# Attention blocks of a fused transformer pair: where a pair's scores, VectorE's maxima and the bias rows stand in their queues

## The chip, the cores and the metric

The kernel runs on one core of one Trainium2 chip. The metric is device time in microseconds (us) of one execution, the median of several. The core has TensorE (PE; its weight loads are listed as PEld), VectorE (DVE), ScalarE (ACT), GpSimd (POOL) and the SyncE queue (SP). Each takes its own queue of instructions in order, and they release each other by semaphores.

## The reference, cut to what matters

Two transformer blocks run one after the other on a sequence of S = 1024 rows of width D = 1024. The second block has a mixer of two halves: a dilated attention (8 heads of width 64) and a diagonal state-space mixer (32 groups of 16 channels, 64 complex states each). The change lies in this mixer alone:

```
for window, dilation in ((128, 1), (512, 4), (2048, 16)):        # dilated_attention
    s = einsum(q, k) * 64 ** -0.5 + bias                         # bias = -slope[h] * distance, masked
    m = max(s); p = exp(s - m); denom = sum(p)
    o = einsum(p, v) / denom;  lse = m + log(denom)
out = sum over branches of softmax(lse) * o

bu = einsum(u, b_bar)                                            # s5_mixer
x_t = a_bar * x_(t-1) + bu_t
y = real(einsum(x, c)) + d_skip * u;  y = gelu(y) * sigmoid(gelu(y) @ w_glu + b_glu)
```

The kernel computes the mixture of the three branches as one softmax: a key that lies in one, two or three of the branches gets a bias of 0, log 2 or log 3 more. So one score matrix, one row maximum and one sum per head are enough.

## The kernel before, in words

The sequence has NT = 8 tiles of 128 rows. A block `n` of the attention is one head and one tile `i` of 128 queries against the `i+1` key tiles up to it, so it is 128 to 1024 wide. There are NA = 64 blocks. `block_of` orders them: heads in pairs, so blocks 2m and 2m+1 are the same tile of two heads, and the tiles of a pair of heads in the order 0, 1, 4, 5, 2, 3, 6, 7. Eight blocks are called a batch here. A batch with tiles 0, 1, 4, 5 is a short batch (blocks of 128, 256, 640 and 768 columns, two of each), one with tiles 2, 3, 6, 7 a long one (384, 512, 896 and 1024). They take turns: short, long, short, and so on, four of each; I call them A0, B0, A1, B1 to A3, B3. Blocks are numbered 0 to 7 within a batch. Four blocks that share an output bank form a group; a batch has two.

One block passes through these steps:
- `scores_pair` (TensorE, L1745) writes the scores of two blocks into banks 0 to 3. It waits for `at_m`, the maxima of the pair before, since these read the same banks.
- `maximum` (VectorE, L1759) adds the head's bias row, writes the negated scores `sco` and their row minimum `stats`, and signals `at_m`. It waits for its scores (`at_s`) and for the turns of the block three before (`at_tr`), which read the same slot of `sco`.
- the exponential (ScalarE, L1843), then `transposes` (TensorE, L1777), the turns of the 128x128 pieces, and `rest` (ScalarE, L1834), which copies them out as `probT` (`at_pt`).
- `values` (TensorE, L1804) multiplies a finished group's `probT` by V into bank 6. The work on a group is cut into four parts, one in each of the next four blocks; the last signals `at_pv`.
- `inverses` (VectorE, L1864 and L1865) takes 1/sum of a group's four blocks and spreads it over 64 columns as `rdw` (`at_r`). `factors` (TensorE, L1787) turns `rdw` into bank 6. `finish` (VectorE, L1872 and L1874) copies that out as `rdb` and multiplies the group's output by it into `att_o` (`at_o`). `factors` of a group waits for its own `inverses` and for `finish` of the group before, whose bank it overwrites.
- `head_bias` (VectorE, L1731) writes one 1024-wide bias row for a head of the next pair.

Between them stand the steps of the state-space mixer: `ssm_step_pe` (TensorE) in block 0 and 1 of a batch turns inputs (L1452), in 2 and 3 multiplies (L1419), in 5 and 6 prepares the next batch (L1460, L1452), and in block 7 multiplies twelve times (L1432 to L1434). VectorE has products in blocks 2 and 3 (L1377, L1379), an add and four scans in block 4 (L1383, L1386), and two products in block 5 (L1394, L1396). ScalarE copies the turns out (L1495) and, behind block 7, the result (L1487).

No scheduler is involved: the order in each queue is the order in which the three loops over `n` in `att_pe`, `att_act` and `att_dve` are written. Up to now TensorE's loop issues the scores of the next pair at the start of each even block, and VectorE's loop issues, at the start of a group, `finish`, then `inverses`, then the maximum, and a bias row behind the maxima of both blocks of tile 5.

Of the kernel before, what the change touches and what calls it, by code (L numbers as in the profile page):

```python
# [8 lines left out]
NT = S // P  # L9
# [9 lines left out]
N_HEADS = 8  # L19
# [25 lines left out]
def program(nc, x, p, stream, cols, rows, gate_mats, pool_mats, inv_count, ssm_g, ssm_bc, x_mid, ssm_mid, att_mid, out):  # L45
# [7 lines left out]
    with ctx:  # L53
# [1626 lines left out]
        ot_hi, ot_lo = sem("ot_hi"), sem("ot_lo")  # L1680
        NA = N_HEADS * NT
        NQ = NA // 4
        BIAS_AT = 5
        TILE_ORDER = (0, 1, 4, 5, 2, 3, 6, 7)
        TURNED_AT = {6: 0, 4: 0, 2: 4 * S, 0: 4 * S}

        def block_of(n):

            pair, r = divmod(n, 2 * NT)
            return 2 * pair + r % 2, TILE_ORDER[r // 2]  # L1690
# [36 lines left out]
        def head_bias(dve, h):  # L1727
            both = dl0 if h < 2 else dl
            if h == 2:
                dve.wait_ge(dl_in, 16)  # L1730
            nc.vector.scalar_tensor_tensor(out=bias_of(h), in0=both[:, 0:S], scalar=-2.0 ** (-(h + 1.0)),  # L1731
                                           in1=both[:, S:2 * S], op0=ALU.mult, op1=ALU.add).then_inc(dve_chain, 1)
            chained["dve"] += 1
            return chained["dve"]
# [15 lines left out]
        def maximum(dve, n, made):  # L1750
            h, i = block_of(n)
            w = (i + 1) * P
            if i == 0:
                dve.wait_ge(dve_chain, made)
            dve.wait_ge(at_s, n + 1)
            if n >= 3:
                dve.wait_ge(at_tr, n - 2)
            b = 2 * (n % 2)
            nc.vector.tensor_tensor_reduce(out=scored(n)[:, 0:w],  # L1759
                                           in0=ps[:, b:b + 2, :].rearrange("p a b -> p (a b)")[:, 0:w],  # L1760
                                           in1=bias_of(h)[:, S - w:S], scale=-1.0, scalar=3e38, op0=ALU.add,
                                           op1=ALU.min, accum_out=nm_[:, n:n + 1]).then_inc(at_m, 1)
# [5 lines left out]
        def att_pe(pe):  # L1768
            def transposes(n):
                i = block_of(n)[1]  # L1770
                pe.wait_ge(at_e, n + 1)
                if n:
                    alone = turn_bank(n) and turn_bank(n - 1)
                    if n > 1 or not alone:
                        pe.wait_ge(at_pt, n - 1 if alone else n)
                for k in range(i + 1):
                    last = nc.tensor.transpose(ps[:, (turn_bank(n) or 4) + k // 4, (k % 4) * P:(k % 4 + 1) * P],  # L1777
                                               scored(n)[:, k * P:(k + 1) * P], ident[:, :])
                last.then_inc(at_tr, 1)

            def factors(q):

                pe.wait_ge(at_r, q + 1)
                if q:
                    pe.wait_ge(at_o, q)
                for a in range(2):
                    nc.tensor.transpose(ps[:, 6, (2 + a) * P:(3 + a) * P],  # L1787
                                        rdw[:, q % 2, 2 * a:2 * a + 2, :].rearrange("p a b -> p (a b)"), ident[:, :])

            def values(q, part):  # L1790

                h, t0 = block_of(4 * q)
                if t0 == 0:
                    steps = [(0, 0, 1, True, True), (0, 1, 2, True, False), (1, 1, 2, False, True)]
                else:
                    steps = [(0, 0, 2, True, False), (t0 + 1, 1, 2, False, False)]
                    steps += [(k, 0, 2, False, k == t0) for k in range(1, t0 + 1)]
                n = len(steps)
                for i in range(part * n // 4, (part + 1) * n // 4):
                    k, a, b, first, last = steps[i]  # L1800
                    if i == 0:
                        pe.wait_ge(at_pt, 4 * q + 4)
                    for r in range(2):
                        ins = nc.tensor.matmul(ps[64 * r:64 * r + 64, 6, a * P:b * P],  # L1804
                                               V[:, k, (h + r) * HEAD_DIM:(h + r + 1) * HEAD_DIM],
                                               turned(q, r)[:, a:b, k, :], start=first, stop=last)
                    if i == n - 1:
                        ins.then_inc(at_pv, 1)

            for n in range(NA):  # L1810
                if n % 2 == 0 and n + 2 < NA:
                    scores_pair(pe, n // 2 + 1)
                if n == 0:
                    pe.wait_ge(u_out, GT)
                transposes(n)
                if n % 4 == 0 and n:
                    factors(n // 4 - 1)
                if n == 0:
                    ssm_turn_pe(pe, 0, 0)
                ssm_step_pe(pe, n)  # L1820
                if n >= 4:
                    values(n // 4 - 1, n % 4)
            factors(NQ - 1)
            for part in range(4):
                values(NQ - 1, part)
# [32 lines left out]
        def att_dve(dve):  # L1858
            link = lambda ins: link_dve(dve, ins)

            def inverses(q):

                dve.wait_ge(at_e, 4 * q + 4)
                link(nc.vector.reciprocal(rd_[:, 4 * q:4 * q + 4], den_[:, 4 * q:4 * q + 4]))  # L1864
                nc.vector.tensor_copy(rdw[:, q % 2, :, :], rd_[:, 4 * q:4 * q + 4].unsqueeze(2).to_broadcast(  # L1865
                    [P, 4, HEAD_DIM])).then_inc(at_r, 1)

            def finish(q):

                h, t0 = block_of(4 * q)  # L1870
                dve.wait_ge(at_pv, q + 1)
                nc.vector.tensor_copy(rdb[:, :], ps[:, 6, 2 * P:4 * P]).then_inc(at_d, 1)  # L1872
                dve.wait_ge(at_d, q + 1)
                nc.vector.tensor_tensor(OT[:, h // 2, t0 * P:(t0 + 2) * P], ps[:, 6, 0:2 * P], rdb[:, :],  # L1874
                                        ALU.mult).then_inc(at_o, 1)

            made = {}
            for n in range(NA):
                if n % 4 == 0 and n >= 8:
                    finish(n // 4 - 2)  # L1880
                if n % 4 == 0 and n:
                    inverses(n // 4 - 1)
                if n + 2 < NA:
                    maximum(dve, n + 2, made.get(block_of(n + 2)[0], 0))
                h, i = block_of(n + 2)
                if i == BIAS_AT and h + 2 < N_HEADS:
                    dve.wait_ge(at_m, n + 3)
                    made[h + 2] = head_bias(dve, h + 2)
                ssm_step_dve(dve, n)
                ssm_rest_dve(dve, n)  # L1890
            finish(NQ - 2)
            inverses(NQ - 1)
            lo_of(dve, glu_unit(0))
            finish(NQ - 1)
            lo_of(dve, glu_unit(1))
# [462 lines left out]
```

## Time and profile before

| | |
|---|---|
| Time, median of 3 runs | 3159.32 us (3157.42 to 3162.17) |
| The profiled execution | 3157.16 us, span 3155.3 us |
| Busy in the span | PE 3036.2 us (96%), PEld 2470.5 (78%), DVE 1376.3 (44%), ACT 869.7 (28%), POOL 411.8 (13%) |
| Granted TensorE clock, mean | 0.989 of full speed |
| The attention loop | about us 2088 to 2286 of the span |

A row of a timeline is a stretch of like instructions of one engine: its start in us from the start of the span, its length, the engine, the line, out<-in, shapes and count; in brackets how long the engine was idle before it and which instruction ended that. Matmuls are pipelined, so a row's length runs a little past the start of the next row.

### The profile page before, as it was taken

What the parts mean: (1) busy time and instruction counts of PE and PEld (TensorE: products, weight loads), DVE (VectorE), ACT (ScalarE), POOL (GpSimd) and SP (SyncE); (2) the same over time, 40 slices, a digit from 0 to 9 for tenths busy, and PEclk for the clock granted to TensorE, in tenths of its full rate; (3) what the DMA queues carried; (4) which work ended last, traced back from release to release, by engine and by line L of the source; (5) the groups of instructions that cost most, each with busy time, mean ns of one, the idle gap of its engine ahead of it and who ended that gap; (6) DMA issues with size and microseconds to landing.
All of it is one profiled execution on the core that took longest, in us unless ns stands there. A gap on an engine that the chain in (4) does not pass through costs nothing. (4 is left out here: it accounts for less than half of the span.)

```text
span 3155.3 us, 36156 instructions
## 1 busy us (share of the span) xinstructions
PE 3036.2 (96%) x13904; PEld 2470.5 (78%) x13904; DVE 1376.3 (44%) x1715; ACT 869.7 (28%) x1313; POOL 411.8 (13%) x1004
## 2 busy tenths in 40 slices
PE   7999999999998989999999999999998999999998
PEld 5767888888886768888888877876677888888886
DVE  5653444444446353433343354335546333333336
ACT  6523211222113252111211133135644211121112
POOL 0001000000000000788870010011100000000000
PEclk9999999999999999999999999999999999999999
DMA  3112111111112022122221132212122111111113
GB/s 125 40 61 80 61 43 44 53 53 53 40 41 67 27 74 67 65 80 87 94 97 40 47 114 87 82 60 71 56 91 105 65 41 47 47 60 47 40 47 127
DMA packets 54405, 206.93 MB, mean 66 GB/s; under 512 B 7216, under 2 KB 7984, under 8 KB 52000
## 3 DMA queue, kind: packets, MB, share of 16 engines
q1 hardware_dynamic: 38592, 140.53, 13.3%
q0 software_dynamic: 15712, 65.02, 5.6%
q8 instruction: 68, 1.11, 0.1%
q14 instruction: 33, 0.27, 0.0%
HBM read 173.15 MB, written 31.20 MB: 65 GB/s over the span
## 5 line engine op out<-in xcount | busy, mean ns | idle before, releaser
L126 PE MATMUL ps<-region_a,region_b 128*128 128x512 f32 x1664 | 658.0, 395 | 18.1 <-DVE region_a L221 9.8
L128 PE MATMUL ps<-region_a,region_b 128*128 128x512 f32 x1664 | 649.9, 391 | 0.0
L127 PE MATMUL ps<-region_a,region_b 128*128 128x512 f32 x1664 | 649.8, 391 | 0.0
L815 DVE TENSOR_TENSOR acc<-acc,ps 128x1024 f32<-128x1024 f32 x288 | 350.9, 1219 | 332.2 <-PE ps L128 332.2
L126 PE MATMUL ps<-region_b,region_a 128*128 128x512 f32 x1088 | 432.6, 398 | 17.3 <-DVE region_b L121 10.0
L127 PE MATMUL ps<-region_b,region_a 128*128 128x512 f32 x1088 | 428.8, 394 | 0.0
L128 PE MATMUL ps<-region_b,region_a 128*128 128x512 f32 x1088 | 428.6, 394 | 0.0
L121 DVE TENSOR_TENSOR region_b<-raw,region_b 128x1024 fp32r<-128x1024 f32 x176 | 218.0, 1254 | 395.3 <-ACT region_b L117 395.1
L126 PEld LDWEIGHTS ps<-region_a,region_b 128*128 128x128 f32 x1664 | 314.2, 189 | 86.3 <-DVE region_b L121 7.3
L128 PEld LDWEIGHTS ps<-region_a,region_b 128*128 128x128 f32 x1664 | 313.7, 189 | 65.8
L127 PEld LDWEIGHTS ps<-region_a,region_b 128*128 128x128 f32 x1664 | 314.2, 189 | 64.8 <-issue 1.7
L126 PE MATMUL ps<-region_b 128*128 128x512 f32 x896 | 351.8, 393 | 3.8 <-DVE acc L815 2.4
L128 PE MATMUL ps<-region_b 128*128 128x512 f32 x896 | 349.4, 390 | 0.0
L127 PE MATMUL ps<-region_b 128*128 128x512 f32 x896 | 349.4, 390 | 0.0
L126 PEld LDWEIGHTS ps<-region_b,region_a 128*128 128x128 f32 x1088 | 215.7, 198 | 61.6 <-issue 10.3
L128 PEld LDWEIGHTS ps<-region_b,region_a 128*128 128x128 f32 x1088 | 215.6, 198 | 41.2
L127 PEld LDWEIGHTS ps<-region_b,region_a 128*128 128x128 f32 x1088 | 215.6, 198 | 39.5
L117 ACT ACTIVATE region_b<-raw 128x1024 fp32r<-128x1024 f32 x176 | 181.4, 1050 | 162.1 <-DMA raw<-stream 130.9
L726 ACT ACTIVATE rtmp<-ps 128x512 f32<-128x512 f32 x88 | 52.7, 599 | 628.2 <-PE ps L128 628.1
L121 DVE TENSOR_TENSOR region_a<-raw,region_a 128x1024 fp32r<-128x1024 f32 x74 | 89.5, 1224 | 256.1 <-ACT region_a L117 256.1
L126 PEld LDWEIGHTS ps<-region_b 128*128 128x128 f32 x896 | 168.8, 188 | 40.6 <-DVE acc L815 3.7
L128 PEld LDWEIGHTS ps<-region_b 128*128 128x128 f32 x896 | 168.6, 188 | 35.3
(290 smaller groups left out, 3204.5 us busy)
## 6 DMA issues: line engine op xcount, KB each, us to landing
raw<-stream SPq DMA_DIRECT2D x252, 512.0 KB, 3.3
ssm_row<-ssm_mid POOLq DMA_DIRECT2D x8, 1632.0 KB, 7.7
x_mid<-acc POOLq DMA_DIRECT2D x24, 512.0 KB, 3.0
ssm_mid<-made_osc POOLq DMA_DIRECT2D x8, 1024.0 KB, 4.3
ssm_mid<-made_out POOLq DMA_DIRECT2D x8, 608.0 KB, 3.3
acc<-x SPq DMA_DIRECT2D x8, 512.0 KB, 8.2
rold<-x POOLq DMA_DIRECT2D x16, 256.0 KB, 3.4
old_a<-x_mid POOLq DMA_DIRECT2D x8, 512.0 KB, 7.2
```

Of the source, the lines that this page charges most:

```text
L117: nc.scalar.activation(slot[:, 0, :], raw[:, odd, :], ACT.Copy).then_inc(hi_done, 1)
L121: nc.vector.tensor_tensor(slot[:, 1, :], raw[:, odd, :], slot[:, 0, :].bitcast(f32), ALU.subtract).then_inc(unit_ready, 1)
L126: nc.tensor.matmul(psum, lhs(0), rhs(0), start=first, stop=False)
L127: nc.tensor.matmul(psum, lhs(0), rhs(1), start=False, stop=False)
L128: return nc.tensor.matmul(psum, lhs(1), rhs(0), start=False, stop=last)
L726: nc.scalar.activation(rtmp[:, half, :], ps[:, up_bank(c, j, half), :], ACT.Silu).then_inc(F.sem["ge"], 1)
L815: nc.vector.tensor_tensor(acc[:, t, :], acc[:, t, :], src, ALU.add).then_inc(F.sem["de"], 1)
```

## The change

Three edits in the two loops:
- TensorE: the scores that used to stand at the start of blocks 0 and 2 of a batch now stand one block earlier, behind the turns of block 7 and of block 1 (`EARLY`), and so in front of that block's state-space step. Those at the start of blocks 4 and 6 stay. `factors` moves behind the state-space step.
- VectorE: at the start of a group the maximum of block n+2 comes first, then `inverses`, then `finish`.
- VectorE: the two bias rows for the next pair of heads leave the middle of the short batch. One now stands in block 7 of the short batch, the other in block 0 of the long one.

```diff
@@ -1680,7 +1680,8 @@
         ot_hi, ot_lo = sem("ot_hi"), sem("ot_lo")
         NA = N_HEADS * NT
         NQ = NA // 4
-        BIAS_AT = 5
+        BIAS_AT = (7, 8)
+        EARLY = (1, 7)
         TILE_ORDER = (0, 1, 4, 5, 2, 3, 6, 7)
         TURNED_AT = {6: 0, 4: 0, 2: 4 * S, 0: 4 * S}
 
@@ -1808,16 +1809,18 @@
                         ins.then_inc(at_pv, 1)
 
             for n in range(NA):
-                if n % 2 == 0 and n + 2 < NA:
+                if n % 2 == 0 and n + 2 < NA and (n == 0 or (n - 1) % NT not in EARLY):
                     scores_pair(pe, n // 2 + 1)
                 if n == 0:
                     pe.wait_ge(u_out, GT)
                 transposes(n)
-                if n % 4 == 0 and n:
-                    factors(n // 4 - 1)
+                if n % 2 and n + 3 < NA and n % NT in EARLY:
+                    scores_pair(pe, (n + 3) // 2)
                 if n == 0:
                     ssm_turn_pe(pe, 0, 0)
                 ssm_step_pe(pe, n)
+                if n % 4 == 0 and n:
+                    factors(n // 4 - 1)
                 if n >= 4:
                     values(n // 4 - 1, n % 4)
             factors(NQ - 1)
@@ -1876,16 +1879,18 @@
 
             made = {}
             for n in range(NA):
+                if n + 2 < NA:
+                    maximum(dve, n + 2, made.get(block_of(n + 2)[0], 0))
+                if n % 4 == 0 and n:
+                    inverses(n // 4 - 1)
                 if n % 4 == 0 and n >= 8:
                     finish(n // 4 - 2)
-                if n % 4 == 0 and n:
-                    inverses(n // 4 - 1)
-                if n + 2 < NA:
-                    maximum(dve, n + 2, made.get(block_of(n + 2)[0], 0))
-                h, i = block_of(n + 2)
-                if i == BIAS_AT and h + 2 < N_HEADS:
-                    dve.wait_ge(at_m, n + 3)
-                    made[h + 2] = head_bias(dve, h + 2)
+                pair, r = divmod(n, 2 * NT)
+                if r in BIAS_AT and 2 * pair + 2 < N_HEADS:
+                    if pair:
+                        dve.wait_ge(at_m, 2 * NT * pair)
+                    h = 2 * pair + 2 + BIAS_AT.index(r)
+                    made[h] = head_bias(dve, h)
                 ssm_step_dve(dve, n)
                 ssm_rest_dve(dve, n)
             finish(NQ - 2)
```

The order of VectorE's queue in the middle (block 4) of a long batch, before. `rdb` and `att_o` are `finish`, `stats<-stats` and `rdw` are `inverses`, `sco` is the maximum of block 6, `m1b` and `yb` the state-space step:

```order
L1872 COPY rdb<-ps 128x256 [waits at_pv]
L1874 TENSOR_TENSOR att_o<-ps,rdb 128x256 [waits at_d]
L1864 RECIPROCAL stats<-stats 128x4 [waits at_e]
L1865 COPY rdw<-stats 128x256 [waits dve_chain]
L1759 ISA sco,stats<-ps,bias_g 128x1024 [waits at_tr,at_s]
L1759 ISA stats 128x1
L1383 TENSOR_TENSOR m1b<-m1b,m2b 128x512 [waits s5_m]
L1386 SCALAR_TENSOR_TENSOR yb<-rho,m1b 128x128 [waits dve_chain]
L1386 SCALAR_TENSOR_TENSOR yb<-rho,m1b 128x128 x3
```

and now:

```order
L1760 ISA sco,stats<-ps,bias_g 128x1024 [waits at_tr,at_s]
L1760 ISA stats 128x1
L1867 RECIPROCAL stats<-stats 128x4 [waits at_e]
L1868 COPY rdw<-stats 128x256 [waits dve_chain]
L1875 COPY rdb<-ps 128x256 [waits at_pv]
L1877 TENSOR_TENSOR att_o<-ps,rdb 128x256 [waits at_d]
L1383 TENSOR_TENSOR m1b<-m1b,m2b 128x512 [waits s5_m]
L1386 SCALAR_TENSOR_TENSOR yb<-rho,m1b 128x128 [waits dve_chain]
L1386 SCALAR_TENSOR_TENSOR yb<-rho,m1b 128x128 x3
```

The maximum is in front of the four instructions of the group, and `inverses` in front of `finish`.

VectorE's queue at the start (block 7 of the short batch, then 0 and 1) of a long batch, before:

```order
L1759 ISA sco,stats<-ps,bias_g 128x384 [waits at_tr,at_s]
L1759 ISA stats 128x1
L1872 COPY rdb<-ps 128x256 [waits at_pv]
L1874 TENSOR_TENSOR att_o<-ps,rdb 128x256 [waits at_d]
L1864 RECIPROCAL stats<-stats 128x4 [waits at_e]
L1865 COPY rdw<-stats 128x256 [waits dve_chain]
L1759 ISA sco,stats<-ps,bias_g 128x512 [waits at_tr,at_s]
L1759 ISA stats 128x1
L1759 ISA sco,stats<-ps,bias_g 128x512 [waits at_tr,at_s]
L1759 ISA stats 128x1
L1759 ISA sco,stats<-ps,bias_g 128x896 [waits at_tr,at_s]
```

and now, with the two bias rows (`bias_h<-dl`) and with the maximum of block 2 first (128x512):

```order
L1760 ISA sco,stats<-ps,bias_g 128x384 [waits at_tr,at_s]
L1760 ISA stats 128x1
L1732 SCALAR_TENSOR_TENSOR bias_h<-dl 128x1024 [waits at_m]
L1760 ISA sco,stats<-ps,bias_g 128x512 [waits at_tr,at_s]
L1760 ISA stats 128x1
L1867 RECIPROCAL stats<-stats 128x4 [waits at_e]
L1868 COPY rdw<-stats 128x256 [waits dve_chain]
L1875 COPY rdb<-ps 128x256 [waits at_pv]
L1877 TENSOR_TENSOR att_o<-ps,rdb 128x256 [waits at_d]
L1732 SCALAR_TENSOR_TENSOR bias_h<-dl 128x1024 [waits at_m]
L1760 ISA sco,stats<-ps,bias_g 128x512 [waits at_tr,at_s]
L1760 ISA stats 128x1
```

The second bias row stands between `finish` and the maximum of block 3, the second 128x512 row.

TensorE's queue at the same place, from the end of block 2's and 3's scores on (`qk` are scores, `ident,sco` turns, `ident,rdw` factors, `probT,v` values), before:

```order
L1745 MATMUL ps<-qk 128x512
L1777 MATMUL ps<-ident,sco 128x128 [waits at_pt,at_e]
L1777 MATMUL ps<-ident,sco 128x128 x2
L1787 MATMUL ps<-ident,rdw 128x128 [waits at_o,at_r]
L1787 MATMUL ps<-ident,rdw 128x128
L1452 MATMUL ps<-ident,ssm_row 128x128 [waits s5_g,s5_cp]
L1452 MATMUL ps<-ident,ssm_row 128x128 x3
L1804 MATMUL ps<-probT,v 64x256 [waits at_pt]
L1804 MATMUL ps<-probT,v 64x256
L1777 MATMUL ps<-ident,sco 128x128 [waits at_pt,at_e]
L1777 MATMUL ps<-ident,sco 128x128 x2
L1452 MATMUL ps<-ident,ub 128x128 [waits ub_made,s5_cp]
```

and now, from the scores that moved in front of the twelve products of block 7 on (left out, with the last values and the turns of block 0):

```order
L1746 MATMUL ps<-qk 128x512 [waits at_m]
L1746 MATMUL ps<-qk 128x512
...
L1452 MATMUL ps<-ident,ssm_row 128x128 [waits s5_g,s5_cp]
L1452 MATMUL ps<-ident,ssm_row 128x128 x3
L1788 MATMUL ps<-ident,rdw 128x128 [waits at_o,at_r]
L1788 MATMUL ps<-ident,rdw 128x128
L1805 MATMUL ps<-probT,v 64x256 [waits at_pt]
L1805 MATMUL ps<-probT,v 64x256
L1778 MATMUL ps<-ident,sco 128x128 [waits at_pt,at_e]
L1778 MATMUL ps<-ident,sco 128x128 x2
L1746 MATMUL ps<-qk 128x512 [waits at_m]
L1746 MATMUL ps<-qk 128x512
```

The first scores are ahead of the state-space products, the factors are behind the turns of `ssm_row`, and the next scores come directly behind the turns of block 1.

## Rows read from the trace of the kernel before

**Rows 1.** TensorE's waits, us 2088 to 2282: line, releaser, us, times, longest.
```profile
PE ps L1745 <- DVE stats L1759: 6.2, 7, 1.7
```

**Rows 2.** Timeline, middle of a long batch: start, us, engine, instruction [wait].
```profile
2171.87 1.99 PE L1745 MATMUL ps<-qk 64*128 64x512 f32 x8
...
2173.89 1.23 DVE L1759 CUSTOM_DVE_ANT_0 sco<-ps,bias_g 128x1024 f32<-128x1024 f32 x1 [0.61 <-PE ps L1745]
...
2174.50 0.25 PEld L1787 LDWEIGHTS ps<-ident,rdw 128*128 128x128 f32 x2
...
2174.92 0.65 PE L1804 MATMUL ps<-probT,v 128*64 128x256 f32 x4
...
2175.04 0.69 DVE L1383 TENSOR_TENSOR m1b<-m1b,m2b 128x512 f32<-128x512 f32 x1
...
2175.87 0.95 PE L1777 MATMUL ps<-ident,sco 128*128 128x128 f32 x7 [0.30 <-ACT probT L1834]
...
2177.17 1.22 DVE L1759 CUSTOM_DVE_ANT_0 sco<-ps,bias_g 128x1024 f32<-128x1024 f32 x1
...
2178.45 0.49 PE L1745 MATMUL ps<-qk 64*128 64x128 f32 x4 [0.28 <-DVE stats L1759]
```

**Rows 3.** Timeline, middle of a short batch.
```profile
2147.62 1.56 PE L1745 MATMUL ps<-qk 64*128 64x512 f32 x8
...
2149.22 0.96 DVE L1759 CUSTOM_DVE_ANT_0 sco<-ps,bias_g 128x768 f32<-128x768 f32 x1 [0.18 <-PE ps L1745]
...
2150.22 1.22 DVE L1731 SCALAR_TENSOR_TENSOR bias_h<-dl 128x1024 f32<-128x1024 f32 x1
...
2151.36 0.68 DVE L1383 TENSOR_TENSOR m1b<-m1b,m2b 128x512 f32<-128x512 f32 x1
...
2154.50 0.92 PE L1745 MATMUL ps<-qk 64*128 64x384 f32 x4 [1.65 <-DVE stats L1759]
```

**Rows 4.** Timeline, start of a short batch.
```profile
2136.93 0.70 PE L1745 MATMUL ps<-qk 64*128 64x256 f32 x4
...
2137.04 0.42 DVE L1872 COPY rdb<-ps 128x256 f32<-128x256 f32 x1 [5.07 <-PE ps L1804]
...
2137.50 0.42 DVE L1874 TENSOR_TENSOR att_o<-ps,rdb 128x256 f32<-128x256 f32 x1
...
2137.84 0.17 DVE L1864 RECIPROCAL stats<-stats 128x4 f32<-128x4 f32 x1
...
2138.34 0.40 DVE L1759 CUSTOM_DVE_ANT_0 sco<-ps,bias_g 128x256 f32<-128x256 f32 x1
...
2138.47 0.44 PE L1787 MATMUL ps<-ident,rdw 128*128 128x128 f32 x2 [0.59 <-DVE rdw L1865]
...
2139.28 0.87 PE L1804 MATMUL ps<-probT,v 128*64 128x256 f32 x8
...
2143.07 0.44 PE L1777 MATMUL ps<-ident,sco 128*128 128x128 f32 x2
```

**Rows 5.** Timeline, start of a long batch, TensorE.
```profile
2161.04 1.13 PE L1745 MATMUL ps<-qk 64*128 64x512 f32 x4
...
2162.10 0.55 PE L1777 MATMUL ps<-ident,sco 128*128 128x128 f32 x3
...
2163.90 0.55 PE L1777 MATMUL ps<-ident,sco 128*128 128x128 f32 x3
...
2167.32 0.66 PE L1777 MATMUL ps<-ident,sco 128*128 128x128 f32 x4
```

**Rows 6.** Timeline, first batch.
```profile
2092.46 1.11 PE L1452 MATMUL ps<-ident,ub 128*128 128x128 f32 x4 [0.58 <-ACT ztb L1495]
...
2096.08 1.06 PE L1419 MATMUL ps<-ztb 128*128 128x128 f32 x8
...
2105.99 0.92 PE L1745 MATMUL ps<-qk 64*128 64x384 f32 x4 [1.69 <-DVE stats L1759]
```

**Rows 7.** Busy us by engine (count), granted clock (PEclk), DMA, one us of it.
```profile
2094.00:2095.00 1.00, 1.00 (x4) 0.34 (x3) 0.00 (x0) 0.69 (x3) 0.66 (x2) 0.50 1.01 418
```

## The prediction

> **What bounds the kernel now.** I read the page first: its groups show TensorE busy for nearly the whole span, so what counts is where TensorE waits, not how busy VectorE is. Next the waits of TensorE in the attention stretch, the only stretch that the change touches: its score products waited for VectorE's maxima seven times, 6.2 us in all [rows 1]. Then the timelines of the four places where instructions move: the middle (block 4) and the start (block 0) of a short batch and of a long one. There are four short batches (A0 to A3) and four long ones (B0 to B3), in turn. TensorE executes its queue in order, so every place is read in the same way: when is TensorE there, and when is VectorE.
>
> **What each place costs now.** In the middle of a long batch TensorE comes to the pair of factor turns at 2174.50 and doesn't wait: VectorE has written both of its group results while the 1024-wide scores ran, from 2171.87 [rows 2]. In the middle of a short batch two bias rows stand in VectorE's queue, the first at 2150.22, and the next scores wait 1.65 us for the second maximum, that of block 7 [rows 3]. At the start of a short batch the factor turns wait 0.59 us [rows 4]. At the start of a long batch nothing waits for long [rows 5].
>
> **Middle of a long batch, the term that decides.** Let S be the start of the scores (2171.87). The 1024-wide maximum starts at S+2.02, because it needs those scores, and VectorE's next instruction at 2175.04, S+3.17 [rows 2]. Before, `inverses` and `finish` ran ahead of that maximum, under the scores. Now they stand behind it. From the copy of `finish` to its multiply are 0.46 us, and from there over the reciprocal and the spread to the next instruction 0.84 [rows 4], together 1.30, which ends at S+4.47. The last instruction of the group is now the multiply, which starts 0.34 before that [rows 4], at S+4.13, takes 0.42 and releases TensorE about 0.05 later (2177.17 + 1.22 against 2178.45 [rows 2]): S+4.60. The factor turns wait for `at_o` as well as `at_r`, so they start at S+4.60 in place of S+2.63: a new wait of 1.97 us. The values follow 0.42 after the factors (2174.50 to 2174.92 [rows 2]) and last 0.58 (0.65 less 0.07 that such rows overlap), so the turns of block 5 start at S+5.60, not S+4.00. From them to the next scores are 2.58 us, 0.28 of them a wait [rows 2], so TensorE is there at S+7.90. VectorE: the add at S+4.47, the second maximum, that of block 7, 2.13 later (2175.04 to 2177.17), 1.22 for it and the lag: S+7.88. Both agree on S+7.90 where it was S+6.58: **+1.32 us**. ScalarE's exponential and copy behind these scores keep their distance to them, so nothing is caught up. The ends: 0 if waits that TensorE has anyway take all of it (0.30 and 0.28 [rows 2] take some), +1.97 if they take nothing. I take the value that both engines' sides give.
>
> **Middle of a short batch.** S is 2147.62. The maximum starts at S+1.60, the next instruction at S+2.60 [rows 3]; the group takes 1.30 as above, so the add stands at S+3.90, where the bias row and the add put it at 2151.36, S+3.74. The removed bias row gave 1.14 (2150.22 to 2151.36), the moved group costs 1.30. The second maximum comes 2.13 later, lasts 0.96, and the scores start at S+7.05 against S+6.88: **+0.17**. The bias row's gain is spent by the group that moved in. In A0 there is no `finish` yet, so 0.46 + 0.34 less: **−0.63**, which takes a part of the 1.69 us wait there [rows 6].
>
> **Start of a short batch.** Let 0 be 2136.93. The scores (0.70, less the overlap 0.63) now lie before the last state-space products of the batch before: the same work, earlier. `finish` copies at +0.11, multiplies at +0.57 and ends at +0.99 [rows 4]; the maximum and the inverses lie before it, under those products. The factors start at +1.05 and the values at +1.47, where they were at +2.35 [rows 4]. With the scores that moved 2.10: **−0.25**. What follows up to 2143.07 keeps its length.
>
> **Start of a long batch.** Let 0 be 2161.04. The same counting gives the values at +1.47, the turns of block 1 at +2.06 and, with the old distance of 3.42 from them to the next turns [rows 5], +5.48; the 1.06 of the moved scores added is 6.54, against 6.28: **+0.26**. In B0 to B2 the second bias row stands right behind `finish`: it starts at +0.91, takes 1.14, the 512-wide maximum about 0.68 (an estimate between the 0.40 for 256 in rows 4 and the 0.96 for 768 in rows 3) and the lag brings +2.79. TensorE now wants that maximum at +2.44, since the next scores come right behind the turns of block 1 (2.06 and 0.38, three turns at 0.55 less overlap): 0.35 more, **+0.61**. Bounds from −0.2 to +1.2, the whole bias row. The first bias row (block 7) runs beside the state-space products and costs nothing; without that cover it would cost 1.14.
>
> **First batch, block 1.** The scores now fill the 0.58 us in which TensorE waited for ScalarE's copy [rows 6]. The least gain is 0.58; the most is 1.7, if the clock, 0.50 of full speed there [rows 7], which is 1.2 GHz, does not fall at all and only the copy of the third turn bounds the products of 2096.08. I take −0.9, nearer to the wait's row.
>
> **The sum.** A0: −0.9 − 0.63 = −1.5. A1 to A3: 3 × (0.17 − 0.25) = −0.2. B0 to B2: 3 × (1.32 + 0.61) = +5.8. B3: 1.32 + 0.26 = +1.6. Together **+5.7 us**. The stages behind start later by as much, as TensorE bounds them too. The profiled execution took 3157.16 us (span 3155.3), so I expect 3162.9 in a like one. The median of the runs is 2.16 us above it: 3159.32 + 5.7 = **3165.0 us**.
>
> The row of the wait for the factors shows the turn itself 0.59 us late [rows 4]. The Trainium skill (TensorE: Matmul & The Clock Gate, "Step-by-step: what each phase is for") says that TensorE can pull weight loads ahead of earlier matmuls while matmuls stay in order. By it the values' first weight load could run inside the new wait. At 0.13 us for a load (0.25 for two [rows 2]) that would be 0.5 us off the four long batches, 3164.5; the sum above leaves it out.
>
> **Rivals.**
> *Faster.* The group behind the maximum is done before TensorE needs it, since the early scores let VectorE run ahead. Then the middles keep only the bias row's gain, 1.65 at most in A1 to A3 and in A0, with −0.25 three times at the start, −0.9 in A0 and +0.26 four times: −6.6 − 0.75 − 0.9 + 1.0 = −7.2, 3152. It decides if the factors at the middle of B start before S+2.7. Against it: these scores are not among the early ones, and the maximum starts 2.02 after them [rows 2]. 6%.
> *Slower still, by the clock.* TensorE's clock has fallen once in this stretch, behind small waits [rows 6, 7]. If it falls after each new 1.97 us wait as it did there (half speed at most from 2092.46 to 2096.08, so at most 1.8 us lost), it is 4 × 1.8 = +7: 3172. Against it: behind waits of 1.65 and 1.69 us the same scores last 0.92 us both times [rows 3, 6], the length at the full clock. 12%.
> *No change.* The new wait overlaps waits that TensorE has anyway, and half of the B term is lost: +2.8 or less, 3162. For it: small waits on ScalarE stand there, 0.30 us [rows 2]. 18%.
> The forecast itself: 64%.
>
> **How the numbers follow.** A change of 0.2%, 6.3 us, is about what a measurement of this kernel can tell from none. My case lies between +3 and +9 and crosses that line: 28 of its 64 points lie above it, 36 below. With the rivals: slower 0.40 (28 and 12), same 0.54 (36 and 18), faster 0.06. The range takes the no-change rival's middle and the clock rival's: 3160 to 3172.
>
> **What would show it.** Right, if in the profile after the factor turns in the middle of each long batch wait about 2 us for `att_o`, written by `finish`, in all four; if the scores behind the middle of a short batch wait 0.5 to 0.7 us for a maximum rather than 1.65; if the factors at a batch's start come 1.05 behind the values; and if the scores of block 1 in the long batches wait about 0.35 us in B0 to B2 and not in B3. Wrong, if the factor turns at the middle don't wait, if the clock falls in a middle, or if VectorE's maximum of block 7 is late by more than 1.4 us.

## The result, and the profile after

The changed kernel takes 3168.0 us, median of 13 runs (3165.95 to 3169.26), against 3158.42 us (3156.24 to 3163.06, 13 runs) for the kernel before: a ratio of 1.0027, 95% interval 1.0019 to 1.0036, so slower by some 8.5 us (9.6 by the two medians). I had forecast 3165.0 and +5.7 us, in a range of 3160 to 3172. The profiled execution took 3169.09 us (span 3167.3).

The waits of TensorE in the attention stretch, after (line, releaser, us, times, longest; us 2080 to 2300), for [rows 1]:

```profile
PE ps L1788 <- DVE att_o L1877: 12.5, 10, 1.7
...
PE ps L1746 <- DVE stats L1760: 3.0, 7, 0.7
...
PE ps L1778 <- ACT probT L1837: 2.4, 9, 0.6
...
PE ps L1788 <- DVE rdw L1868: 2.2, 2, 1.4
```

Two lines of the same view before:

```profile
PE ps L1777 <- ACT probT L1834: 7.0, 17, 1.2
...
PE ps L1787 <- DVE rdw L1865: 3.0, 4, 1.4
```

The waits of the scores for a maximum have halved, from 6.2 to 3.0 us, and those of the turns for ScalarE's copy shrank from 7.0 to 2.4. In their place stands a wait that did not exist before: the factors for `att_o`, which `finish` writes, ten times, 12.5 us. Before, they waited for `rdw` alone, 3.0 us in all.

The middle of the first long batch, B0 (start, us, engine, instruction, wait), for [rows 2]:

```profile
2123.49 1.99 PE L1746 MATMUL ps<-qk 64*128 64x512 f32 x8
...
2125.50 1.23 DVE L1760 CUSTOM_DVE_ANT_0 sco<-ps,bias_h 128x1024 f32<-128x1024 f32 x1 [2.10 <-PE ps L1746]
...
2126.65 0.17 DVE L1867 RECIPROCAL stats<-stats 128x4 f32<-128x4 f32 x1
...
2127.07 0.42 DVE L1875 COPY rdb<-ps 128x256 f32<-128x256 f32 x1
...
2127.52 0.42 DVE L1877 TENSOR_TENSOR att_o<-ps,rdb 128x256 f32<-128x256 f32 x1
...
2127.86 0.68 DVE L1383 TENSOR_TENSOR m1b<-m1b,m2b 128x512 f32<-128x512 f32 x1
...
2128.09 0.41 PE L1788 MATMUL ps<-ident,rdw 128*128 128x128 f32 x2 [1.70 <-DVE att_o L1877]
...
2128.43 0.20 PEld L1805 LDWEIGHTS ps<-probT,v 128*64 128x64 f32 x4 [0.17 <-issue]
...
2129.01 0.98 PE L1778 MATMUL ps<-ident,sco 128*128 128x128 f32 x7
...
2129.98 1.23 DVE L1760 CUSTOM_DVE_ANT_0 sco<-ps,bias_h 128x1024 f32<-128x1024 f32 x1
...
2131.27 0.49 PE L1746 MATMUL ps<-qk 64*128 64x128 f32 x4
```

With S = 2123.49: the multiply starts at S+4.03 (forecast 4.13), the factors at S+4.60 (4.60), the turns of block 5 at S+5.52 (5.60), the next scores at S+7.78 (7.90), where they stood at S+6.58: +1.20 us, forecast +1.32.

The same place in the second long batch, B1:

```profile
2178.74 0.41 PE L1788 MATMUL ps<-ident,rdw 128*128 128x128 f32 x2 [1.70 <-DVE att_o L1877]
...
2179.90 1.76 PE L1778 MATMUL ps<-ident,sco 128*128 128x128 f32 x7
...
2181.59 1.61 PE L1460 MATMUL ps<-ssm_row 128*16 128x128 f32 x8
...
2183.50 0.49 PE L1746 MATMUL ps<-qk 64*128 64x128 f32 x4
```

The wait is the same, but now seven turns take 1.76 us and not 0.98, the eight products 1.61 and not 1.05, and the scores come 4.76 us behind the factors in place of 3.18. The granted clock (PEclk, the third column from the right) in two stretches behind that wait and in the two that answer to them in B2, where the same wait stands:

```profile
2180.00:2181.00 1.00, 1.00 (x5) 1.00 (x6) 0.96 (x3) 0.00 (x0) 0.00 (x0) 0.50 0.00 0
2181.00:2182.00 1.00, 1.00 (x7) 0.55 (x6) 1.00 (x3) 0.30 (x1) 0.00 (x0) 0.50 0.00 0
2232.00:2233.00 1.00, 1.00 (x9) 0.82 (x10) 0.96 (x4) 0.10 (x1) 0.00 (x0) 1.00 0.05 16
2233.00:2234.00 1.00, 1.00 (x12) 0.69 (x10) 1.00 (x1) 0.94 (x2) 0.00 (x0) 1.00 0.00 0
```

In B1 the clock is at its lower level (0.50, 1.2 GHz) behind a wait of 1.70 us; in B2 it stays at 2.4 GHz behind a wait of 1.70 us.

The middle of a short batch, A1, for [rows 3], and the factors at the start of that batch and the scores of block 1 at the start of B0, for [rows 4, 5]:

```profile
2149.06 1.56 PE L1746 MATMUL ps<-qk 64*128 64x512 f32 x8
...
2152.97 0.41 PE L1788 MATMUL ps<-ident,rdw 128*128 128x128 f32 x2 [1.66 <-DVE att_o L1877]
...
2155.89 0.92 PE L1746 MATMUL ps<-qk 64*128 64x384 f32 x4 [0.61 <-DVE stats L1760]
...
2140.23 0.41 PE L1788 MATMUL ps<-ident,rdw 128*128 128x128 f32 x2 [0.25 <-DVE att_o L1877]
...
2115.83 1.77 PE L1746 MATMUL ps<-qk 64*128 64x512 f32 x8 [0.18 <-DVE stats L1760]
```

The scores come at S+6.83 with S = 2149.06 (before 6.88, forecast 7.05). The factors at the start wait 0.25 us, before 0.59; the scores in B0's block 1 wait 0.18 for the maximum behind the bias row.

To add up the stretch I take the first turn of block 0 in each batch, up to the first turn behind the last (L1541). The time of each batch in us:

| | A0 | B0 | A1 | B1 | A2 | B2 | A3 | B3 | sum |
|---|---|---|---|---|---|---|---|---|---|
| before | 24.21 | 23.97 | 24.54 | 23.96 | 24.46 | 23.96 | 23.20 | 28.12 | 196.42 |
| after | 21.98 | 26.04 | 24.60 | 27.62 | 24.60 | 26.05 | 24.60 | 30.79 | 206.28 |
| difference | −2.23 | +2.07 | +0.06 | +3.66 | +0.14 | +2.09 | +1.40 | +2.67 | +9.86 |
| forecast | −1.5 | +1.93 | −0.08 | +1.93 | −0.08 | +1.93 | −0.08 | +1.58 | +5.7 |

The stretch carries 9.9 of the 11.9 us between the two profiled executions; 1.7 of the rest lie ahead of it, where nothing was changed. These two executions lie further apart than the medians: the one before is 1.3 us below its median, the one after 1.1 above.

### The profile page after: what moved, and what is told of

The parts are those of the page before. It is cut to its first block, busy times and chain, and to the rows that moved or that the text cites. A ratio compares the mean times of both kernels' runs of the same rounds, so it can differ in the third digit from the quotient of the medians.

```text
span 3167.3 us, 36155 instructions
## 1 busy us (share of the span) xinstructions
PE 3044.2 (96%) x13904; PEld 2473.3 (78%) x13904; DVE 1375.5 (43%) x1715; ACT 868.0 (27%) x1313; POOL 411.0 (13%) x1004
## 4 chain that ended last, share of the span: by engine, by line
PE 92%; DVE 5%; ACT 2%; issue 1%; DMA 0%; SPq 0%; DVEq 0%; ACTq 0%
PE ps L126 28%; PE ps L128 28%; PE ps L127 28%; PE ps L262 1%; PE ps L1746 1%; PE ps L1805 1%; PE ps L1778 1%; DVE acc L815 1%; DVE region_b L121 1%; PE ps L1419 0%; DVE acc L177 0%; DVE acc L185 0%; ACT region_b L117 0%; DVE sco L1760 0%; DVE region_a L221 0%
```

## The experiments

Ratios are to the kernel before, run on the same chip. The sum is that of the table above, from each one's profile. It says more than the time of one execution: the work ahead of the stretch is the same in all twelve profiles, and still the stretch starts anywhere from us 2085.9 to 2091.1. All are cut from the changed kernel or from the one before as said. Theory: VectorE's group behind the maximum in the middles makes the loss, with the clock that sometimes falls behind the new wait. Rivals: the early scores; the bias rows.

### e1: the middles as before

In the changed kernel, VectorE's loop:

```diff
+                if n % 8 == 4:
+                    if n >= 8:
+                        finish(n // 4 - 2)
+                    inverses(n // 4 - 1)
                 if n + 2 < NA:
                     maximum(...)
-                if n % 4 == 0 and n:
-                    inverses(n // 4 - 1)
-                if n % 4 == 0 and n >= 8:
-                    finish(n // 4 - 2)
+                if n % 8 == 0 and n:
+                    inverses(n // 4 - 1)
+                    finish(n // 4 - 2)
```

> The changed kernel, but at block 4 of each batch VectorE has finish and inverses ahead of the maximum again, as before the change. Theory (the group behind the maximum in the middles is the cost, with the fall of the clock that sometimes follows): the waits of 1.70 and 1.66 us of the factors for att_o go, and with them 1.2 us in each of B0 to B3, 1.2 in A1 to A3, 0.4 in A0 and the slow matmuls of B1 and B3: 9 to 11 us below the changed kernel, 3157 to 3159, no slower than the kernel before. Rival one (the early scores are the cost): at most 2 us less than the changed kernel, 3166. Rival two (the bias rows' new places): no change either, 3168.

3157.11 us, ratio 0.9990 (0.9981 to 0.9999), sum 194.85: 11.4 us less than the changed kernel's sum. Its waits:

```profile
PE ps L1788 <- DVE att_o L1877: 0.8, 3, 0.3
...
PE ps L1746 <- DVE stats L1760: 3.0, 10, 0.4
```

Of the waits for `att_o` 0.8 us are left, at the starts of the short batches, and the clock falls nowhere in the eight batches. The order in the middles carries the whole loss and more.

### e2: the bias rows back

```diff
-        BIAS_AT = (7, 8)
+        BIAS_AT = 5
-                if r in BIAS_AT and 2 * pair + 2 < N_HEADS:
-                    ...
+                h, i = block_of(n + 2)
+                if i == BIAS_AT and h + 2 < N_HEADS:
+                    dve.wait_ge(at_m, n + 3)
+                    made[h + 2] = head_bias(dve, h + 2)
```

> The changed kernel, but both bias rows stand in the middle of the short batch again, behind the group and behind the second maximum. Theory: the middles of A0 to A2 get 1.14 us more each before the scores of block 0, and the 0.18 us wait in the long batches' block 1 goes: +3 us on the changed kernel, 3171. Rival two (the new places are what costs): 3 us or more below the changed kernel, 3165 or less. Rival one: no change.

3174.76 us, ratio 1.0048 (1.0034 to 1.0062), sum 212.41. The direction is as expected, the size is twice as large: +6.8 us on the changed kernel, not +3. The middle of A1:

```profile
2155.32 0.41 PE L1788 MATMUL ps<-ident,rdw 128*128 128x128 f32 x2 [1.66 <-DVE att_o L1877]
...
2159.36 0.92 PE L1746 MATMUL ps<-qk 64*128 64x384 f32 x4 [1.74 <-DVE stats L1760]
```

The scores wait 1.74 us in place of 0.61, the 1.1 expected, in three batches. In A2, where the clock stays up, the batch grows by 1.50: 1.14 at these scores, and 0.36 in block 7, where the early scores now wait 0.29 us for a maximum. More is the clock: this profile has it at 0.50 behind four middles (A0, B0, A1 and B1), the changed kernel's behind two (B1 and B3). A1, with a fall, takes 27.03 us, A2, with the same waits up to it and none, 26.10; B0 and B1 take 27.37 and 27.32, B2 25.79. So a fall cost 0.9 to 1.6 us here.

### e3: no early scores

```diff
-        EARLY = (1, 7)
+        EARLY = ()
```

> The changed kernel, but no scores are early: all stand at the start of an even block as before. Theory: the middles stay as they are, and now at the start of a batch too the group stands behind a maximum that has to wait for its scores, so the factors come about 1.4 us later in the long batches and 0.6 in the short ones, and the 1.7 us of A0's block 1 are lost: +6 to +9 us on the changed kernel, 3174 to 3177. Rival one (the early scores are the cost): faster than the changed kernel by 3 us or more, 3165 or less.

3169.25 us, ratio 1.0033 (1.0021 to 1.0046), sum 209.92, short batches A1 to A3 25.0, long ones 26.45 (B0, where the clock fell behind the middle, 27.97). The start of B1, the turn of the factors:

```profile
2164.41 0.41 PE L1788 MATMUL ps<-ident,rdw 128*128 128x128 f32 x2 [1.17 <-DVE att_o L1877]
```

The factors do wait there (1.17 us), and block 0 of a long batch grows by 1.0 us; but block 1 gives back 0.4 and block 7 0.2, so that a batch grows by only 0.4 us. The rival, that the early scores are the loss, is out: without them the kernel is not faster. My own size was wrong too: +1.3 us by the medians and +3.6 in the stretch, where I had said 6 to 9. Under the new order of VectorE the early scores are worth 0.4 us a batch.

### e4: TensorE's part alone

In the changed kernel, VectorE's loop and the bias rows as before; TensorE's loop and `EARLY = (1, 7)` stay. The lines of the bias rows change as in e2.

```diff
-        BIAS_AT = (7, 8)
+        BIAS_AT = 5
-                if n + 2 < NA:
-                    maximum(...)
-                if n % 4 == 0 and n:
-                    inverses(n // 4 - 1)
                 if n % 4 == 0 and n >= 8:
                     finish(n // 4 - 2)
+                if n % 4 == 0 and n:
+                    inverses(n // 4 - 1)
+                if n + 2 < NA:
+                    maximum(...)
```

> TensorE's part of the change alone (early scores, factors behind the state-space step); VectorE's order and the bias rows as before. Theory: no middle changes; A0 gains 1.7 us in block 1, the long batches' starts lose 0.6 to 0.9 us each and the short ones' about 0.2: 0 to +4 us on the kernel before, 3158 to 3162. Rival one (the early scores carry the loss): +8 us or more on the kernel before, 3166 or more.

3165.59 us, ratio 1.0019 (1.0010 to 1.0028), sum 201.68: +7.3 us by the medians, +5.3 in the stretch. That lies between the two theories, and the interval alone, +3.2 to +8.8, excludes neither. The middles are as before, but A1 takes 25.44 (before 24.54), B1 24.99 (23.96), where I had counted about 0.2 and 0.6 to 0.9. So TensorE's part costs something by itself, more than I had worked out. This run does not say which half of it; e9 and e10 take the early scores and the later factors apart on another base. Some of its waits belong to this mixture alone: the early scores in block 7 of A1 wait 0.29 us for a maximum, behind the bias rows that still stand in the middle, and the factors at the start of the long batches 0.36 for `rdw`. The changed kernel has neither.

### e5: only the inverses behind the maximum

```diff
+                if n % 8 == 4 and n >= 8:
+                    finish(n // 4 - 2)
                 if n + 2 < NA:
                     maximum(...)
                 if n % 4 == 0 and n:
                     inverses(n // 4 - 1)
-                if n % 4 == 0 and n >= 8:
+                if n % 8 == 0 and n:
                     finish(n // 4 - 2)
```

> The changed kernel, but in the middles finish stands ahead of the maximum and only inverses behind it. Theory (both signals count, and the last of them sets the factors): the factors now wait for rdw, about 1.1 us in the middles of the long batches instead of 1.7, so 0.4 to 0.6 us stay of the 1.2; in the short ones the turns of block 5 hide it. The clock no longer falls: 1 to 3 us above the version with the old middle, 3158 to 3160. Rival (only finish, through at_o, costs anything): as fast as that version, 3157, with no wait of the factors.

3161.29 us, ratio 1.0010 (1.0001 to 1.0019), sum 198.11, of long batches 25.25 (e1: 24.84, changed kernel 26.05). The middle of B1:

```profile
2175.61 0.44 PE L1788 MATMUL ps<-ident,rdw 128*128 128x128 f32 x2 [0.82 <-DVE rdw L1868]
```

The factors wait 0.82 us for `rdw`. I had said 1.1; the loss of 0.4 in a long batch against e1 is as expected, and the clock did not fall. But the short batches lose as much (23.81 against 23.40), where I had expected that the turns would hide it, and the median lies 1.3 us above my range. The rival, that `finish` alone matters, is out: whichever of the two signals is last sets the factors.

### e6: the group later still

```diff
                 if n + 2 < NA:
                     maximum(...)
-                if n % 4 == 0 and n:
+                if n % 8 == 0 and n:
                     inverses(n // 4 - 1)
-                if n % 4 == 0 and n >= 8:
                     finish(n // 4 - 2)
                 ...
                 ssm_rest_dve(dve, n)
+                if n % 8 == 4:
+                    inverses(n // 4 - 1)
+                    if n >= 8:
+                        finish(n // 4 - 2)
```

> The changed kernel, but in the middles inverses and finish stand also behind the state-space add and the four scans, 2.1 us later. Theory: the factors' wait in the middles grows from 1.7 to 3.8 us, and 1.3 to 2.1 us more are lost in each of the eight: +13 to +15 us, and as the clock follows TensorE's waits it falls in nearly every middle, 1.6 us each, up to +10 more: 3182 to 3192. Rival (TensorE's wait is mostly hidden by something else that is late): less than +6 us, 3174. Rival (the clock has nothing to do with the new wait): +13 to +15 and two falls as in the changed kernel, 3182.

3194.92 us, ratio 1.0118 (1.0102 to 1.0133), sum 233.92. B1's middle:

```profile
2188.66 0.66 PE L1788 MATMUL ps<-ident,rdw 128*128 128x128 f32 x2 [3.84 <-DVE att_o L1877]
...
2190.30 1.75 PE L1778 MATMUL ps<-ident,sco 128*128 128x128 f32 x7
...
2191.98 1.89 PE L1460 MATMUL ps<-ssm_row 128*16 128x128 f32 x8
```

The wait is 3.84 us and the turns behind it take 1.75. The clock is at 0.50 behind all eight middles, for 3 to 4 us in the short batches and 7 in the long ones (10 in B3), of which some 1.5 us lie inside the wait. It came out 3 us above the range that I had given. For 2.1 us more of wait the short batches grew by 3.0 us and B0 and B2, where the changed kernel had no fall, by 4.5; how this divides between the wait and the clock no run here shows, but in the long batches the clock stays low for twice as long as in the falls from which I had taken my price. The rival without the clock (3182) and the one without an effect (3174) are both out.

### e7: the bias rows' part alone

The kernel before, with the changed kernel's bias rows (the rest of their lines left out):

```diff
-        BIAS_AT = 5
+        BIAS_AT = (7, 8)
-                h, i = block_of(n + 2)
-                if i == BIAS_AT and h + 2 < N_HEADS:
-                    ...
+                pair, r = divmod(n, 2 * NT)
+                if r in BIAS_AT and 2 * pair + 2 < N_HEADS:
+                    ...
```

> The kernel before with the bias rows' part of the change alone (one in block 7, one in block 0 of the long batch). Theory: the scores behind the middles of A0, A1 and A2 wait 0.4 instead of 1.65 us, nothing else moves: 3.7 us less than before, 3154 to 3156. Rival (the bias row in block 0 delays the maxima of the long batch as much): no change, 3158.

3153.73 us, ratio 0.9986 (0.9977 to 0.9995), sum 192.77. The middle of A1:

```profile
2153.49 0.92 PE L1745 MATMUL ps<-qk 64*128 64x384 f32 x4 [0.40 <-DVE stats L1759]
```

0.40 us is left of the 1.65. B0 to B2 stay at 23.96: the bias row in block 0 costs them nothing when the scores that block 2 issues at its start are not moved into block 1.

### e8: what the runs pointed to

The kernel before with three edits (the lines of the bias rows as in e7):

```diff
-        BIAS_AT = 5
+        BIAS_AT = (7, 8)
-                if n % 2 == 0 and n + 2 < NA:
+                if n % 2 == 0 and n + 2 < NA and n != 2:
                     scores_pair(pe, n // 2 + 1)
                 ...
                 transposes(n)
+                if n == 1:
+                    scores_pair(pe, 2)
                 ...
+                if n % 4 == 0 and n:
+                    inverses(n // 4 - 1)
                 if n % 4 == 0 and n >= 8:
                     finish(n // 4 - 2)
-                if n % 4 == 0 and n:
-                    inverses(n // 4 - 1)
                 if n + 2 < NA:
                     maximum(...)
```

> The kernel before with the bias rows at their new places, the scores of block 2 early in the very first batch alone, and VectorE's group ahead of the maximum as before, but with inverses in front of finish. Theory: 3.7 us for the bias rows, 1.5 for the first batch (its clock doesn't fall), 0.4 at each of the three later starts of a short batch: 6 to 7 us less than before, 3151 to 3153. Rival (what TensorE gains in this stretch is lost again in a later wait): within 3 us of the kernel before.

3151.09 us, ratio 0.9978 (0.9969 to 0.9987), sum 189.67: A0 21.40, short batches 22.86, long ones 23.89. The factors at the start of A1 and the scores behind its middle:

```profile
2136.83 0.41 PE L1787 MATMUL ps<-ident,rdw 128*128 128x128 f32 x2 [0.19 <-DVE att_o L1876]
...
2151.58 0.92 PE L1745 MATMUL ps<-qk 64*128 64x384 f32 x4 [0.40 <-DVE stats L1759]
```

0.19 in place of 0.59, and 0.40 in place of 1.65. It beats both kernels, as expected.

### e9 and e10: early scores, and later factors, on e8

e9 gives e8 the changed kernel's conditions for `scores_pair`, e10 moves `factors` alone:

```diff
-                if n % 2 == 0 and n + 2 < NA and n != 2:        # e9
+                if n % 2 == 0 and n + 2 < NA and (n == 0 or (n - 1) % NT not in (1, 7)):
-                if n == 1:
-                    scores_pair(pe, 2)
+                if n % 2 and n + 3 < NA and n % NT in (1, 7):
+                    scores_pair(pe, (n + 3) // 2)
```

```diff
-                if n % 4 == 0 and n:                            # e10
-                    factors(n // 4 - 1)
                 ssm_step_pe(pe, n)
+                if n % 4 == 0 and n:
+                    factors(n // 4 - 1)
```

> The best version (e8) with the changed kernel's early scores in every batch, and nothing else of it. Theory after the first runs (early scores cost by themselves: they break up runs of like instructions, 0.1 to 0.3 us each, and ask for a maximum sooner): +0.3 to 0.5 us a batch, 3153 to 3155. Rival (they cost only together with VectorE's new order): as fast as e8 or faster by what they fill, 3150 to 3151.

> The best version (e8) with the factors behind the state-space step, and nothing else of the change. Theory: at the start of a short batch the turns of the state-space inputs fill the 0.19 us wait for att_o, at the start of a long one a run of turns is broken up for about as much: within 1 us of e8. Rival (this is what made TensorE's part slow): +0.3 us or more at each of seven starts, 3153 or more.

e9: 3160.47 us, ratio 1.0010 (1.0001 to 1.0019), sum 199.7, short batches 23.83, long ones 25.45. That is 9.4 us slower than e8 by the medians, which are of two chips, and 10.0 in the stretch, far more than the 0.3 to 0.5 a batch that I expected. The factors at the start of A1 and of B1 in e9, and the scores of B1's block 1:

```profile
2138.43 0.41 PE L1787 MATMUL ps<-ident,rdw 128*128 128x128 f32 x2 [0.82 <-DVE att_o L1876]
...
2162.26 0.41 PE L1787 MATMUL ps<-ident,rdw 128*128 128x128 f32 x2 [0.60 <-DVE att_o L1876]
...
2164.52 1.77 PE L1745 MATMUL ps<-qk 64*128 64x512 f32 x8 [0.36 <-DVE stats L1759]
```

They wait 0.82 and 0.60 us for `att_o`, where e8 waits 0.19 and nothing. The scores that used to stand between the last values and the factors were the cover under which `finish` ran; issued one block earlier they leave it bare. About 0.6 us in each batch is that, and 0.36 more in B0 to B2 the wait for the maximum in block 1; of the 1.5 in A0 1.3 go with the clock, which fell there in this execution and not in e8's.

The rest, 0.3 us in a short batch and 0.6 in a long one, can be read from starts of rows. The turns in front of the factors of B1, in e8 with the factors behind them, and in e9:

```profile
2159.18 0.55 PE L1777 MATMUL ps<-ident,sco 128*128 128x128 f32 x3
2159.56 0.38 PE L1787 MATMUL ps<-ident,rdw 128*128 128x128 f32 x2
...
2161.11 0.55 PE L1777 MATMUL ps<-ident,sco 128*128 128x128 f32 x3
```

In e8 the factors start 0.38 us behind the turns, in e9 1.15 (2161.11 to 2162.26): 0.77 more for a wait that is listed as 0.60. A wait is counted from the end of the row ahead, and without a wait the next row starts some 0.17 before that end. So each new wait of a long batch costs 0.17 more than its length. The first products of the state-space step in block 7 of A1, in e8 and in e9, where the scores stand in front of them:

```profile
2154.98 0.39 PE L1432 MATMUL ps<-toep,ztb 128*128 128x128 f32 x2
2155.20 0.39 PE L1433 MATMUL ps<-ssm_row,ob 128*128 128x128 f32 x2
...
2157.87 0.49 PE L1432 MATMUL ps<-toep,ztb 128*128 128x128 f32 x2
2158.19 0.39 PE L1433 MATMUL ps<-ssm_row,ob 128*128 128x128 f32 x2
```

From the first pair of products to the second are 0.22 us in e8 and 0.32 behind the scores. The turns in front of the scores take 0.1 more as well. So scores that cut a run of 128x128 matmuls in two cost 0.20 us in block 7 and 0.15 in block 1 without any wait. For a short batch that gives 0.63 + 0.20 + 0.15 = 0.98 us, measured 0.97; for a long one 0.60 + 0.36 + 2 × 0.17 + 0.20 + about 0.06 for the cut in block 1 = 1.56, measured 1.56.

e10: 3150.25 us, ratio 0.9975 (0.9966 to 0.9984), sum 188.54, short batches 22.48. The start of A1 in e10:

```profile
2135.38 0.60 PE L1452 MATMUL ps<-ident,ssm_row 128*128 128x128 f32 x4
...
2135.82 0.38 PE L1787 MATMUL ps<-ident,rdw 128*128 128x128 f32 x2
```

The factors no longer wait: the turns of the state-space inputs (L1452) now cover `finish`. That is 0.4 us at the start of A1 to A3. It came out within 1 us of e8, as expected, and the rival, that the later factors made TensorE's part slow, is out. The interval of e10 overlaps that of e8.

## Why the prediction came out as it did

**The place and the mechanism held.** The step that decided, the group behind a maximum that has to wait for its scores, was shown by undoing it (e1, the loss gone), by halving it (e5) and by enlarging it (e6). In the middle of B0 the chain of S+4.60, S+5.60 and S+7.90 came out as 4.60, 5.52 and 7.78. The factors start where I had put them; the wait reads 1.70 and not 1.97, since it is counted from the end of the turns' row and I had counted from the start of the weight load at S+2.63. The second maximum came 1.19 us late, within the 1.4 that I had allowed. The factors at a batch's start come 1.15 behind the values (to the start of the row that follows these), forecast 1.05.

**The totals agree better than the terms.** B0 and B2 lost 2.07 and 2.09 for a forecast of 1.93: 1.21 in the middle (1.32) and 0.87 in blocks 0, 1 and 7 (0.61). A1 and A2 came out at +0.06 and +0.14 for −0.08, and that is luck: the middle gave −0.04 (+0.17) and the rest +0.11 to +0.19 (−0.25), two errors of opposite sign. The bias rows taken out of A0 to A2 were worth 1.25 us each (e7), not 1.14.

**The wait in block 1 of the long batches** is 0.18 in B0 to B2 and absent in B3, forecast 0.35 and absent. **The first batch** gained 2.23 for 1.5: the clock did not fall in block 1, and the products of block 2 started 1.66 us sooner, so the gain there was my upper bound of 1.7 and not the 0.9 that I took. Of the nine profiles with early scores in block 1 (after, e1, e2, e4 to e6, e8 to e10) it fell there in one, e9; of the three without (before, e3, e7) in all.

**A3 was mis-sized: +1.40, forecast −0.08.** The step "middle of a short batch" set the moved group, 1.30, against the removed bias row, 1.14. But only A0 to A2 had a bias row; A3 has no next pair of heads. There the scores waited only 0.40 us before:

```profile
2250.09 0.92 PE L1745 MATMUL ps<-qk 64*128 64x384 f32 x4 [0.40 <-DVE stats L1759]
```

and the group's cost came without its counterpart. I multiplied by three batches of which one was of another kind; the code's condition `h + 2 < N_HEADS` says it.

**The clock was a rival at 12% and came in in part.** My own list had a fall in a middle as a sign of being wrong, and it came. It fell in two of the eight middles of the profiled execution, and cost 1.6 us in B1 (27.62 against 26.05 in B2) and about 1.0 in B3 (30.79 against 29.76 in e2, which is alike there and had no fall). Its argument against, that waits of 1.65 us had left the clock alone, was true of the profile before and too narrow: of the seven middles with a wait for `att_o` of 1.66 to 1.71 us it fell in two (after), in one (e3) and in three (e2), and with waits of 2.9 to 3.8 us (e6) in all eight. In e2 it also fell in A0, which has a wait of 0.78 there; the falls of A0 and A1 in e2 began only behind a second wait, of 1.81 and 1.74 us, and A2 had the same two waits and no fall. What decides between like places no run here shows.

**The early scores' own cost was missed.** I counted the moved scores as the same work at another time. In the changed kernel block 7 grew by 0.20 us in all batches but the last and block 1 by 0.15 where nothing waits, and e9 against e8 shows where it comes from: cut runs, and the cover that `finish` lost. In the changed kernel they still pay (e3: 0.4 us a batch), because there the group stands behind a maximum that then finds its scores ready: at the start of B1 the factors wait 1.17 us without the early scores and less than 0.1 with them.

**The weight loads did not run ahead.** I had left out 0.5 us for loads of the values inside the new wait, and rightly: in B0 the first of them starts at 2128.43, with the values and 0.34 behind the factors that had waited.

**The sum.** Forecast +5.7. To it come A0 −0.7, A3 +1.5, the clock +2.6 (1.6 and 1.0) and 0.1 to 0.2 in each of the others, +0.9: the +9.9 of the profile. The median moved by 8.5 to 9.6; the interval of the ratio is +6.0 to +11.4, so the forecast of +5.7 was too small, for A3, the clock and the early scores. On the three chances: the result is slower by 0.27%, above the line, to which I had given 0.40, less than to no change.

## What to carry to other kernels

When one engine's queue is reordered, look for what the moved instruction used to hide: a maximum put ahead of short group work delays that work by its own wait for its input, and a product moved earlier leaves bare what ran under it. Price a reordering place by place with the first start of each instruction and check for each place that it exists in every turn of the loop. Where two edits of a change lie on the same chain, run each alone: here the bias rows alone were worth about 4 us (e7), and the rest of the change cost some 13 on top of them. And a batch's total that agrees with the forecast says little while the places inside it have not been compared.

## What the runs showed of the hardware that was not expected

A wait of 1.70 us in front of the same matmuls was followed by a fall of the clock from 2.4 to 1.2 GHz in B1 and not in B2 of one execution. The falls behind the middles of after and e2 lasted 3 to 4 us, as in A0 of the kernel before; in e6's long batches 7 and more. One cost 0.9 to 1.6 us. Without a fall the wait of 1.70 us cost 1.2 us of span (B0 of e1 against after), since later waits shrank; with a fall it cost 2.8 (B1).

In the first batch the clock fell to 0.50 in block 1 in the three profiles without early scores there, where waits of 0.82, 0.69 and 0.58 us stand close together, and in one of the nine with them, where only the first two of these waits stand.

A wait costs 0.17 us more than the profile lists for it where the row behind it would otherwise have started before the end of the row ahead, and a score product that cuts a run of 128x128 matmuls in two costs 0.15 to 0.20 us (e9 against e8).
